# Attention of a two-layer block rebuilt: row-group scores, bias on VectorE, Fourier between the heads

## The reference, cut to what matters

```
s = einsum('bqhcd,bkhcd->bhcqk', q, k) * 32**-0.5 - slope[h] * |qpos - kpos|     # slope[h] = 2**-(h+1)
p = softmax(s); a = p[:, :, 0] - lam * p[:, :, 1]
o = a @ v; o = o * rsqrt(mean(o*o) + 1e-5) * subln_g * (1 - lam_init)            # per head of 64
f = real(fft(fft(u_group, features), tokens)) @ w_f + b_f
mix = concat(o, f) @ w_o; h = layer_norm(ALPHA * h + mix); h = layer_norm(ALPHA * h + swiglu(h))
```

## Time and profile before

| | us |
|---|---|
| median of 3 runs (1282.0 to 1287.17) | 1285.35 |
| profiled execution, its time | 1290.82 |
| its span | 1288.9 |
| mean granted PE clock | 0.976 |

### The profile page before, as it was taken

The page is one execution under the profiler, slowest core; times in us unless marked ns, Lnnn a source line. Parts: engine busy times, 40 slices in busy tenths (PEclk is TensorE's granted clock), DMA queues, the critical chain, the costliest instruction groups (busy, mean ns, idle before and its releaser), DMA issues.

```text
span 1288.9 us, 20446 instructions
## 1 busy us (share of the span) xinstructions
PE 1222.7 (95%) x8124; PEld 1103.8 (86%) x8124; DVE 837.1 (65%) x1023; ACT 548.9 (43%) x625; POOL 107.9 (8%) x95
## 2 busy tenths in 40 slices
PE   5998899999899989999996999999999998999997
PEld 4885799999787669999985999997898997999996
DVE  6674767777676658677758477776558557644444
ACT  4453444344244325443433433433487535443342
POOL 3200340000050006000000000000000000000000
PEclk9999999999898999999997999998999999999999
DMA  9610366777361114677761567772532553555550
GB/s 369 255 66 33 117 243 231 278 289 284 124 229 66 66 66 166 226 272 281 293 261 56 211 228 288 287 271 94 196 131 99 174 186 131 196 195 182 179 193 33
DMA packets 34931, 243.08 MB, mean 189 GB/s; under 512 B 3808, under 2 KB 5232, under 8 KB 8256
## 3 DMA queue, kind: packets, MB, share of 16 engines
q1 hardware_dynamic: 27792, 196.03, 41.2%
q0 software_dynamic: 5600, 45.56, 9.9%
q10 hardware_dynamic: 1488, 0.76, 0.2%
HBM read 241.29 MB, written 1.05 MB: 188 GB/s over the span
## 4 chain that ended last, share of the span: by engine, by line
PE 82%; DVE 9%; ACT 4%; issue 3%; DMA 1%; POOL 0%; SPq 0%; DVEq 0%; ACTq 0%
PE bank L407 74%; PE bank L541 2%; DVE x_lo L1091 2%; ACT w_hi L756 1%; DVE w_lo L1018 1%; PE bank L517 1%; PE bank L561 1%; DVE small L1034 1%; DVE x_hi L1089 1%; PE bank L523 1%; DMA raw<-stream 1%; DVE h L1047 1%; PE bank L481 1%; PE bank L573 1%; DVE h L1067 1%
## 5 line engine op out<-in xcount | busy, mean ns | idle before, releaser
L1018 DVE TENSOR_TENSOR w_lo<-raw,w_hi 128x2048 fp32r<-128x2048 f32 x184 | 432.4, 2355 | 225.5 <-ACT w_hi L756 225.4
L407 PE MATMUL bank<-x_hi,w_hi 128*128 128x256 f32 x1824 | 521.0, 286 | 5.2 <-DVE x_lo L1091 1.8
L407 PE MATMUL bank<-x_lo,w_hi 128*128 128x256 f32 x1824 | 517.6, 284 | 0.0
L407 PE MATMUL bank<-x_hi,w_lo 128*128 128x256 f32 x1824 | 517.5, 284 | 0.0
L756 ACT ACTIVATE w_hi<-raw 128x2048 fp32r<-128x2048 f32 x184 | 350.9, 1908 | 188.9 <-PE bank L407 180.0
L407 PEld LDWEIGHTS bank<-x_hi,w_hi 128*128 128x128 f32 x1824 | 349.5, 192 | 12.6 <-issue 5.1
L407 PEld LDWEIGHTS bank<-x_lo,w_hi 128*128 128x128 f32 x1824 | 349.5, 192 | 1.6
L407 PEld LDWEIGHTS bank<-x_hi,w_lo 128*128 128x128 f32 x1824 | 349.3, 192 | 0.0
L407 PE MATMUL bank<-w_hi,hid_hi 128*128 128x512 f32 x352 | 141.5, 402 | 0.0
L407 PE MATMUL bank<-w_hi,hid_lo 128*128 128x512 f32 x352 | 139.2, 396 | 0.0
L407 PE MATMUL bank<-w_lo,hid_hi 128*128 128x512 f32 x352 | 138.6, 394 | 0.0
(11 more groups left out here) (156 smaller groups left out, 1197.2 us busy)
## 6 DMA issues: line engine op xcount, KB each, us to landing
raw<-stream SPq DMA_DIRECT2D x184, 1024.0 KB, 4.8
work<-ada POOLq DMA_DIRECT2D x24, 1536.0 KB, 7.7
gain_rows<-rows POOLq DMA_DIRECT2D x11, 512.0 KB, 6.7
gate_rows<-rows POOLq DMA_DIRECT2D x3, 512.0 KB, 11.6
h<-x SPq DMA_DIRECT2D x4, 256.0 KB, 4.7
out<-z SPq DMA_DIRECT2D x4, 256.0 KB, 2.1
c<-consts SPq DMA_DIRECT2D x1, 960.0 KB, 12.7
wf<-w_f ACTq DMA_DIRECT2D x2, 256.0 KB, 14.0
```

The costliest lines, as they stand in the source:

```text
L407: last = nc.tensor.matmul(out, stationary, moving, start=start and i == 0, stop=stop and i == 2, skip_group_check=True)
L1018: nc.vector.tensor_tensor(w_lo[j % SLOTS][:, :], raw[j % SLOTS][:, :], w_hi[j % SLOTS][:, :].bitcast(F32), ALU.subtract).then_inc(lo_ready, 1)
```

## The change

- The stream is reordered: V0, V1, U0, U1, Q0, K0, Q1, K1; U is projected in 24 passes of 512 columns into B[2:4].
- `scores(p)` does two heads, thus four maps, at once: eight f32 products of 32 rows, each map in its own group of 32 rows and its own bank of B[4:8], the first token half of all four and then the second. The bias product is gone, and the bf16 constants with it.
- `add_bias(h)` on DVE adds the distances to the scores, scales them and finds the row extreme, in four instructions a head (256 columns each, PSUM and SBUF in, SBUF out, with an accumulator output). q is scaled by -(32**-0.5) * 2**(h+1) to that end, so the map is kept negated. The exponentials now work in SBUF.
- `combine(h)` is a reciprocal, a product of 2 columns and two instructions of 256 columns; the first map isn't divided by its sum, and the head's normalisation makes up for it (`head_variance`).
- The copy of the transposed map moves from DVE to ACT (`keep_aT`), with two buffers.
- `w_f` is multiplied into the Fourier matrices once a layer (`fourier_tables`, two products of 512 columns): before the layer's input transposes in layer 1, after V1 in layer 0. A group then has two stages, and the groups are spread between the heads.
- Heads are normalised in two fours; the root is taken on POOL (`head_roots`, 8 columns). O0 and O1 are done tile by tile between the last heads.
- The modulation buffer shares space with the attention's, so the first tile of each feed-forward part is loaded only after the residual stream of that part.

Lines added and context of the core:

```diff
+V0, V1, U0, U1, Q0, K0, Q1, K1, O0, G0 = 0, 1, 2, 3, 4, 5, 6, 7, 8, 12
...
-        SCORES = [B[2], B[3], B[7]]
         RES = B[4:8]
+        SCORES = B[4:8]
...
+            def head_roots(l):
+
+                for f in range(2):
+                    pool.wait_ge(head_var_ready, 2 * l + f + 1)
+                    nc.gpsimd.tensor_tensor(head_rstd[:, f, :], head_var[:, f, :], neg_half, ALU.pow)\
+                        .then_inc(head_rstd_ready, 1)
+
+            def ada_tiles(f):
+
+                first = ADA_STEPS * f
+                pool.dma_start(ada_raw, ada[first]).then_inc(ada_landed, 16)
...
-            pool.dma_start(ada_raw, ada[0]).then_inc(ada_landed, 16)
             for l in range(DEPTH):
                 residual_stream(2 * l)
                 load_gain_rows(2 * l + 1)
+                head_roots(l)
...
+                def scores(p):
+
+                    for m in range(2):
+                        for u in range(4):
+                            if p >= 1 and m == 0:
+                                pe.wait_ge(biased, 16 * l + 4 * (p - 1) + u + 1)
+                            r = HD * u
+                            last = nc.tensor.matmul(SCORES[u][:, m * S:(m + 1) * S],
+                                                    qT[r:r + HD, p, m * P:(m + 1) * P], kT[r:r + HD, p, :],
+                                                    start=True, stop=True, skip_group_check=True)
+                            if m == 1:
+                                last.then_inc(scores_done, 1)
 
                 def transpose_a(h):
+                    bank = B[3] if h < 4 else B[0]
...
+                def fourier_tables(banks):
+
+                    pe.wait_ge(consts_landed, 16)
+                    pe.wait_ge(wf_landed, 16 * DEPTH)
+                    for c, part in ((0, cos_c), (1, neg_sin_c)):
+                        nc.tensor.matmul(banks[c][:, :], part, wf[l][:, :, :].rearrange("p g n -> p (g n)"),
+                                         start=True, stop=True).then_inc(tables_done, 1)
...
                 def fourier_features(g):
                     pe.wait_ge(P_ready, 4 * l + (g + 1))
+                    for c in range(2):
+                        last = nc.tensor.matmul(B[1][:, 0:S], tables[:, c, g * P:(g + 1) * P],
+                                                P_s[:, c * S:(c + 1) * S], start=c == 0, stop=c == 1)
+                    last.then_inc(y_done, 1)
...
+                        pe.wait_ge(mix_a_ready, 2 * l + (k // 2 + 1))
+
+                def mixed_row(i, tile):
+
+                    to_residual(t, O0 + i, mix_hi, mix_lo, (tile - tile % 2, tile - tile % 2 + 1), i == 0, False,
+                                mixed_tile, rows=(tile % 2,))
+
+                if l > 0:
+                    pe.wait_ge(gates_kept, 2 * l)
+                    fourier_tables(B[0:2])
+                transposes(2 * l)
+                if l > 0:
+                    pe.wait_ge(tables_kept, 2 * l + 2)
+                for c in range(2):
+                    token_projection(t, V0 + c, B[0:2], c, input_tile(2 * l))
+                if l == 0:
+                    fourier_tables(B[6:8])
+                for c in range(2):
+                    token_projection(t, U0 + c, B[2:4], c, input_tile(2 * l))
+                pe.wait_ge(proj_evac, 8 * l + 2)
+                projection(t, Q0, B[0], x_hi, x_lo)
+                projection(t, K0, B[1], x_hi, x_lo)
+                pe.wait_ge(proj_evac, 8 * l + 5)
+                projection(t, Q1, B[0], x_hi, x_lo, ks=range(0, 2))
+                pe.wait_ge(proj_evac, 8 * l + 6)
+                pe.wait_ge(tables_kept, 2 * l + 2)
+                scores(0)
+                projection(t, Q1, B[0], x_hi, x_lo, ks=range(2, 7))
+                scores(1)
+                transpose_a(0)
+                projection(t, Q1, B[0], x_hi, x_lo, ks=range(7, 8))
+                fourier_tokens(0)
+                values(0)
+                transpose_a(1)
+                pe.wait_ge(proj_evac, 8 * l + 7)
+                projection(t, K1, B[0], x_hi, x_lo, ks=range(0, 2))
+                values(1)
+                fourier_features(0)
+                projection(t, K1, B[0], x_hi, x_lo, ks=range(2, 4))
+                transpose_a(2)
+                projection(t, K1, B[0], x_hi, x_lo, ks=range(4, 6))
+                values(2)
+                transpose_a(3)
+                fourier_tokens(1)
+                projection(t, K1, B[0], x_hi, x_lo, ks=range(6, 8))
+                values(3)
+                fourier_features(1)
+                pe.wait_ge(proj_evac, 8 * l + 8)
+                scores(2)
+                fourier_tokens(2)
+                fourier_features(2)
+                scores(3)
+                transpose_a(4)
+                transpose_o(0)
+                fourier_tokens(3)
+                values(4)
+                transpose_a(5)
+                fourier_features(3)
+                values(5)
+                pe.wait_ge(biased, 16 * l + 16)
+                mixed_row(0, 4)
+                transpose_a(6)
+                mixed_row(0, 5)
+                values(6)
+                transpose_a(7)
+                mixed_row(1, 6)
+                values(7)
+                mixed_row(1, 7)
+                to_residual(t, O0 + 2, mix_hi, mix_lo, (0, 1), False, False, mixed_tile)
+                transpose_o(1)
+                to_residual(t, O0 + 3, mix_hi, mix_lo, (2, 3), False, True, mixed_tile)
...
                 def exps(h):
                     for c in range(2):
+                        act.wait_ge(biased, 16 * l + 2 * h + c + 1)
                         for m in range(2):
+                            p = probs[:, h % 3, c, m, :]
+                            last = nc.scalar.activation(p, p, ACT.Exp, bias=neg_max[:, h % 3, c, m:m + 1], scale=-1.0,
+                                                        accum_out=sums[:, h, c, m:m + 1])
                         last.then_inc(probs_ready, 1)
+
+                def keep_aT(h):
+                    bank = B[3] if h < 4 else B[0]
+                    act.wait_ge(aT_done, 8 * l + (h + 1))
+                    if h >= 2:
+                        act.wait_ge(o_done, 8 * l + (h - 1))
+                    nc.scalar.activation(aT_s[:, h % 2, :, :].rearrange("p k n -> p (k n)"), bank[:, :], ACT.Copy)\
+                        .then_inc(aT_ready, 1)
...
+                keep_tokens(V1, v_s)
+                split(t, 4)
+                if l == 0:
+                    keep_tables(B[6:8])
+                split(t, 5)
+                keep_tokens(U1, u_s)
+                split(t, 6)
+                act.wait_ge(consts_landed, 16)
+                keep_query(Q0)
+                split(t, 7)
+                keep_key(K0)
+                exps(0)
+                exps(1)
+                keep_aT(0)
+                keep_query(Q1)
                 keep_P(0)
+                exps(2)
+                keep_aT(1)
+                mix_fourier(0)
+                exps(3)
+                split(t, 8)
+                keep_aT(2)
+                keep_aT(3)
                 keep_P(1)
+                keep_key(K1)
+                mix_fourier(1)
+                head_squares(0)
+                split(t, 9)
+                exps(4)
                 keep_P(2)
+                exps(5)
+                mix_fourier(2)
+                exps(6)
+                keep_aT(4)
+                mix_attention(0)
                 keep_P(3)
+                exps(7)
+                keep_aT(5)
+                mix_fourier(3)
+                keep_aT(6)
+                split(t, 10)
+                keep_aT(7)
+                head_squares(1)
+                split(t, 11)
+                split(t, 12)
+                mix_attention(1)
+                split(t, 13)
                 input_full(2 * l + 1, *layer_columns(l, LN1_G, LN1_B))
+                split(t, 14)
...
+                def add_bias(h):
+
+                    for c in range(2):
+                        u = 2 * (h % 2) + c
+                        dve.wait_ge(scores_done, 16 * l + 2 * h + c + 1)
+                        if h >= 3:
+                            dve.wait_ge(aT_done, 8 * l + (h - 2))
+                        for m in range(2):
+                            last = nc.vector.tensor_tensor_reduce(
+                                out=probs[:, h % 3, c, m, :], in0=SCORES[u][:, m * S:(m + 1) * S], in1=dist[:, m, :],
+                                scale=2.0 ** -(h + 1), scalar=HUGE, op0=ALU.add, op1=ALU.min,
+                                accum_out=neg_max[:, h % 3, c, m:m + 1])
+                        last.then_inc(biased, 1)
+
+                def combine(h):
+
+                    dve.wait_ge(probs_ready, 16 * l + 2 * h + 2)
+                    nc.vector.reciprocal(inv_sums, sums[:, h, 1, :]).then_inc(inv_ready, 1)
+                    dve.wait_ge(inv_ready, 8 * l + h + 1)
```

(64 more changed lines are left out.)

362 lines of the change are left out of this document (97 added, 265 removed).

## The result

The changed kernel takes 1268.3 us in the median of 4 runs (1266.8 to 1269.4), the kernel before 1286.3 beside it on the same chip (1282.0 to 1289.0, 4 runs). The ratio is 0.984, with a 95% interval of 0.981 to 0.987: faster by 18 us by the medians and by 21 by the ratio (17 to 25). The forecast was 1271 in a range of 1262 to 1283. The profiled execution took 1267.4 us, span 1265.7, so the two profiled executions lie 23 us apart, 5 more than the medians.

A forecast was written before the change was run, and what follows sets the result against it. PE was taken to bound the kernel. Gains of 8.8 us in layer 1 and 7.1 in layer 0 sum to 15.9, less 1.7 for the clock 14.2: median 1285.35 to 1271, range 1262 to 1283.

The forecast's parts named there:

- Bound and place of the gain: PE in the mixer, busy 95% of the span: a product saved is worth its time if nothing behind arrives late.
- the walk: Mixer, PE, ACT and DVE lists: each instruction starts once engine and inputs are ready; 93.5 us for the old 94.5.
- fourier_features(2): Layer 1 mixer: PE's largest wait, 5.0 us, for keep_P(2) on ACT behind splits 8 and 9 and head 4's softmax.
- DVE's split 12: End of the mixer: runs until 0.6 us after O3's first bank is summed, so the residual is DVE's.
- Scores: PE in the mixer: eight score products of two heads in some 2.2 us, against 4.2 one after the other.
- Bias instruction: New add_bias instruction on DVE, 32 times a layer: 0.5 us each, bounds 0.4 and 0.7, 2.0 a head.
- Clock: PE in the mixer: more and longer waits bring one more half-clock stretch, a loss of 1.7 us.
- Root on POOL: Root for eight columns: 0.9 us, bounds 0.64 and 5.1; 3 us change nothing, 5.1 add 2.1 a layer.
- No overlap (1): Rival, chance 0.2: score row groups don't overlap, still 0.53 us a product; gain 5.4 less 1.7, 1281 to 1282.
- DVE sets the pace (2): Rival, chance 0.12: the new DVE instruction takes 0.7 us; 1278.6, or 1283 with roots of 5.1 us.
- Slower by the clock (3): Rival, chance 0.09: PE's clock falls for most of the stage; 28 us more slow eats the gain, 42 gives 1292.
- More overlap (4): Rival, chance 0.11: all four maps together and the new instruction at 0.4; 12.0 us a layer instead of 8.8, 1264.

The follow-up runs named there:

- the order test: Changed kernel with only the order of a call's eight score products changed, both token tiles of one map next to each other: 1269.3 us, ratio 0.984.
- the doubled instruction: Changed kernel with each bias and row-minimum instruction on DVE issued once more, into cells nobody reads: 1282.0 us, ratio 0.994.
- the five extra products: Changed kernel with five products of 512 columns that nobody reads in PE's wait before fourier_features(2): 1263.1 us, ratio 0.980.
- both tests of the walk's slopes: Two runs against the changed kernel: all four maps in one row group, 1292.6 us; each bias instruction on DVE issued twice, 1282.0 us.

## Why the prediction was right

**Bound and place of the gain: right.** The stage is the mixer, and the waits came one by one where the walk put them. Forecast and measured, layer 1: values(1) 0.35, 0.43; transpose_a(2) 1.0, 0.60; values(2) 0.5, 0.61; transpose_a(3) 2.1, 1.68; fourier_features(2) 5.0, 5.38; transpose_o(0) 1.75, 1.15; values(5) 0.9, 0.98; O3 1.76, 1.66. They sum to 12.5 where 13.4 were forecast. DVE's split 12 does end after O3's first bank, as forecast. From V1, O0 comes 21.5 us earlier than before and O3 16.5 earlier, where the forecast had some 15 and 9 to 10; before's half clock is some 5 of that, the rest is the two terms that follow.

**Scores: the largest term mis-sized.** Forecast 2.2 us a call, measured 1.08, the lower bound; serial it is 3.98, so four groups run 3.7 times as fast. Taking half, for the two instructions of a float32 product, was the error; the order test shows that nothing waits for a neighbour's group. The Trainium skill ("TensorE: Matmul & The Clock Gate", Part 3) gives 3.07 for four products of 32 rows. The trace shows more, 3.7. In the walk this term is worth 2.9 us a layer.

**Bias instruction: mis-sized.** Forecast 0.5, measured 0.345, under the lower bound of 0.4, which I had from another instruction with an operand in PSUM. In the walk 2.2 us a layer; the doubled instruction, some 4 us a layer without the clock where the walk has 6.6, makes it rather 1.3. With both prices the walk starts O3 at 454.7 instead of 458.75, a gain of 13.4 in layer 1 instead of 8.8 without the clock.

**Clock: length right, sign wrong.** I charged one more stretch than before, 1.7 us. By length that is what came: 13.6 us at half clock in the two mixers, where before had 10.2, all in layer 1. By worth it isn't: before's cost 5.1, the changed kernel's 1.9 in each layer by the five extra products, since they begin inside the wait. With the 2.5 us that the clock and the tables gave between the stages, that makes a gain of 3.8 where I had put a loss of 1.7. Layer 1: 13.4 + 5.1 - 1.9 = 16.6, measured 16.2. Layer 0: 7.1 + 4.6 - 1.9 = 9.8, measured 9.7. These sums fit better than their terms are known: both tests of the walk's slopes (7.6 and 6.6 us a layer) left less to the queues, 5 to 6 and some 4. The Trainium skill ("TensorE: Matmul & The Clock Gate", Part 1) says that waits between bursts bring the clock down. The filled gap agrees with it (1.00 instead of 0.50), the 20.5 us at half clock with PE busy for 19.8 do not.

**Root on POOL: size wrong, verdict right.** 1.66 us, forecast 0.9; the walk has 3 us free there, and with 1.67 it ends at the same time.

**Missing from the sum:** 0.9 us that the start of layer 1 gained, 1.6 by the clock just before it, and 5.0 lost outside the mixer, for which I had nothing. So the profile's sum is 26 in the stages, 2.5 more between them and 5 back, 23, where 14 were forecast. The medians differ by 18 only, since the profiled execution of before stood 4.5 us over its median and that of the changed kernel 1 under. The forecast was right within its range; that it was only 3 us off is partly luck, since its errors in the scores, the bias and the clock, all on the side of too little gain, were partly paid back by a loss outside that it did not foresee.

**The rivals.** No overlap (1): it didn't come; the kernel with one row group for all maps shows what it would have been, 1292.6 instead of the 1281 to 1282 that the rival had, since the clock falls with it. DVE sets the pace (2): no, the instruction is cheap, though a third or more of any excess would reach the end. Slower by the clock (3): the mechanism is real, 6.8 us a layer and not 42 in both. More overlap (4): that is what happened inside the stage; its 1264 was missed by 4, about the loss outside.

## What to carry to other kernels

Ask of the longest wait what it is for, and move what stands in front of that; the copy that the waiting product waits for can be moved ahead with hardly any effect (of 5.4 us of wait 4.7 went and 0.5 us a layer was gained, while moving two splits out of ACT's and DVE's way to the softmax gave 8 us a layer). Weight splits that fit before their use anywhere belong behind the softmax, not in it: with these moves and half a block of work set behind the last transposes the kernel is at 1243.7 us. Small products in separate row groups can be counted at the price of one group, in either of the two orders tried here. And a gain of 2 us in a stage is read from a common instruction behind which the two traces differ by the edit alone, since stretches at half clock elsewhere move a stage by as much.

## What was not expected of the hardware

Float32 products on separate groups of 32 rows overlap almost fully, 1.08 us for eight instead of 3.98, and equally when products of one group are issued back to back (1.10). A product ran ahead of one that stands before it in the list but whose row group was busy. With all products in one group layer 0 had 20.5 us at half clock although PE was busy for 19.8 of them; in layer 1 the same list had 10.2 in the whole stage, so what brought it isn't shown. Work that nobody reads, 4.3 us in a wait of 5.4, made each layer 1.9 us faster by keeping the clock. The 512-column passes of the down-projections slowed by 1.8% in a kernel whose code there is the same; where their buffers begin was ruled out, and the cause isn't known.
